# Two reorderings in one kernel: pair sums taken on VectorE before the sums with ones, and rope and root pieces taken before the next softmax step

## Chip, cores and metric

The kernel runs on one core of a Trainium2 chip. The metric is the time of one execution on the device, in microseconds (us). The engines are called by their short names: PE (TensorE, matrix products), ACT (ScalarE, activations), DVE (VectorE, elementwise), POOL (GpSimd), SP (SyncE, here only the queue that brings weights).

## What is computed

Two blocks of two layers each run on one 1024 x 1024 float32 matrix x (1024 tokens). A layer of the first block normalizes, projects, and joins three branches; a layer of the second block joins a convolution branch, a latent attention branch and a gated unit. Cut to what matters here:

```python
def hybrid_layer(x, ...):                       # first block, 2 layers
    h = rms_norm(x, norm_g); proj = h @ w_in
    # 4 heads, two score maps each, rope on part of q and k
    sc = einsum('bhcqd,bhckd->bhcqk', rotate(q), rotate(k))
    p = softmax(where(mask, sc, NEG_INF)); w = p[:, :, 0] - lam * p[:, :, 1]
    a = rms_norm(w @ v, subln_g) * (1 - lam_init) * silu(az)
    ...
def _layer(x, ...):                             # second block, 2 layers
    y = causal_conv31(a * sigmoid(a_glu)) + conv_b           # 256 channels
    y_conv = (silu(layer_norm(y)) @ pw_w + pw_b) * silu(z_conv)
    v = layer_norm(gelu(v)); y_sg = gelu(u) * mix(v) * silu(z_sg)   # 256 channels
    y = concat([rms_norm(y_conv), rms_norm(y_mla), rms_norm(y_sg)])
    return x + y @ w_out
```

## The kernel before

**Layout.** Activations lie channels first: 128 channels on the partitions, 1024 tokens along the row. A branch of 256 channels is thus two tiles of 128x1024. A sum over channels, which every norm needs, is a matmul with a matrix of ones, which adds over the 128 partitions and leaves the sum on all of them.

**Projections.** Each weight matrix is cut into panels of 1024x128. SP brings a panel, POOL splits it into a high and a low float32r part (lines 443 and 446), and PE multiplies in three passes (lines 477 for half the tokens, 496 for all of them). A panel for all tokens is 48 matmuls, one for half of them 24. Two panels are held at a time; PE's first matmul of a panel tells POOL that the other buffer may be overwritten.

**Order.** All orders are written out by hand: each engine runs its own program, and semaphores join them. In the first block's attention the loop runs over 4 heads h and 8 query tiles q. In step (h, q) PE computes the scores of the next step (lines 717, 722), then "pieces" of other work listed in B1_SLOTS, then the value products at q = 4 (line 765), then waits for `mixed` and transposes the mixed probabilities (line 701), then more pieces. Pieces are half projections of the next head's q, k and v, the gate z, and "ss", the sum of squares of a finished head's half (line 754). Pieces and transposes go in turn through a ring F of three PSUM banks. PE can fill a bank only after its last reader has freed it.

The readers are these. For q and k, DVE's `piece`: shuffle from PSUM (line 1274), product with the cosines from PSUM (line 1276, this frees the bank), product of the shuffled copy with the sines (line 1278), and their sum (line 1281). For "ss", ACT's `piece`: logarithm from PSUM (line 996, frees the bank) and exponential (line 998); DVE's part is lines 1289 and 1293. For the softmax: DVE's `maxima` (line 1253) from PSUM, ACT's `exps` (line 974), DVE's `mix` (lines 1261 to 1265), which signals `mixed`. The pieces q, k and ss that stand behind the transposes of a step are kept in a list `late` and are taken by DVE and ACT in the next step, behind `maxima` and behind `exps`.

**Second block.** After the conv panels PE runs six pair sums per layer among the panels: "cmean" and "smean" over the two tiles of conv output YC and gated input VG, "cvar" and "svar" over their squares, "cbn" and "sbn" over the squares of the two branches' outputs. Each is `pair_sum`: the two tiles one after the other into the same PSUM buffer of a ring T with two buffers. ACT writes the squares (line 2040 and 2041, semaphore sq2) and takes the roots (lines 2030 and 2033). DVE centres (lines 2303, 2305), scales (line 2293), and adds latent squares (line 2335). `total` is the same sum for one tile.

Of the kernel before, what the change touches and what calls it, by code (L numbers as in the profile page):

```python
# [33 lines left out]
HALF = SEQ // 2  # L34
# [491 lines left out]
def first_block(env):  # L526
# [3 lines left out]
    with ExitStack() as ctx:  # L530
# [424 lines left out]
        def scalar(act):  # L955
# [55 lines left out]
            def attention(L):  # L1011
# [220 lines left out]
        def vector(dve):  # L1232
# [34 lines left out]

            def piece(L, use):
                kind, h, half = use
                c, psF = slice(half * HALF, (half + 1) * HALF), bank(use)  # L1270
                if kind in ("q", "k"):
                    dst = (AQ if kind == "q" else AK)[h % 2][:, c]
                    dve.wait_ge(*F.filled(L, use))
                    step(dve.stream_shuffle(ROT, psF, exchange(8)))
                    scale = SCALE if kind == "q" else 1.0
                    dve.scalar_tensor_tensor(out=dst, in0=psF, scalar=scale, in1=rope[:, 0, c], op0=ALU.mult,  # L1276
                                             op1=ALU.mult).then_inc(F.freed(use), 1)
                    step(dve.scalar_tensor_tensor(out=ROT, in0=ROT, scalar=scale, in1=rope[:, 1, c], op0=ALU.mult,
                                                  op1=ALU.mult))
                    dve.wait_ge(*F.drained(L, use))  # L1280
                    dve.tensor_tensor(dst, dst, ROT, ALU.add).then_inc(rotated.sem, 1)
                    dve.wait_ge(*rotated.upto(L, rotations(h, kind, half)))
# [18 lines left out]
            def attention(L):  # L1301
# [11 lines left out]
                for h in range(HEADS):  # L1313
                    for q in range(NT):
                        mix(L, h, q)
                        if q + 1 < NT:
# [291 lines left out]
def second_block(env):  # L1608
# [3 lines left out]
    with ExitStack() as ctx:  # L1612
# [56 lines left out]
        kr_sq = Tally(sem("kr_sq"), 1)  # L1669
# [13 lines left out]
        SQ_C, SQ_S = [X[:, 4], X[:, 5]], [X[:, 6], X[:, 7]]  # L1683
        ROOT, ROOT_C, ROOT_S = ypad[:, 0, PAD:], wk[:, 8], wk[:, 10]
# [71 lines left out]
        def tensor(pe):  # L1756
# [25 lines left out]

            def pair_sum(L, use, tiles):

                pe.wait_ge(*T.room(L, use))
                full(psT[:, T.buf(use)], ones[:], tiles[0], True, False)
                full(psT[:, T.buf(use)], ones[:], tiles[1], False, True).then_inc(T.filled_sem, 1)
# [145 lines left out]
            for L in range(DEPTH):  # L1933
# [4 lines left out]

                pe.wait_ge(*conv_done.upto(L, 2))
                pair_sum(L, "cmean", [YC[:, 0], YC[:, 1]])  # L1940
                pe.wait_ge(*A.drained(L, ("v", 1)))
                pair_sum(L, "smean", [VG[:, 0], VG[:, 1]])
# [4 lines left out]
                pe.wait_ge(*sq2.upto(L, 2))  # L1947
                pair_sum(L, "svar", SQ_S)
# [12 lines left out]
                pe.wait_ge(*sq2.upto(L, 3))  # L1961
                pair_sum(L, "cbn", SQ_C)
# [21 lines left out]
                pe.wait_ge(*sq2.upto(L, 4))  # L1984
                pair_sum(L, "sbn", SQ_S)
# [301 lines left out]
        def vector(dve):  # L2287
# [199 lines left out]
            for L in range(DEPTH):  # L2487
# [23 lines left out]
                for m in (0, 1):  # L2511
                    dve.wait_ge(*A.filled(L, ("pw", m)))
                    dve.scalar_tensor_tensor(out=ZC[:, m], in0=psA[:, A.buf(("pw", m))], scalar=col(C2.pwb + m),
                                             in1=ZC[:, m], op0=ALU.add, op1=ALU.mult).then_inc(A.freed(("pw", m)), 1)
                dve.wait_ge(*T.filled(L, "wgt"))
# [3 lines left out]
                    .then_inc(T.freed("wgt"), 1)  # L2519
                for t in (0, 1):  # L2520
# [212 lines left out]
```

## Time and profile before

| | before |
|---|---|
| median of 3 runs | 3786.62 us (3783.96 to 3786.62) |
| profiled execution | 3790.16 us |
| its span, first to last instruction | 3788.3 us |
| PE matmul busy | 3653.4 us, 96% |
| DVE busy | 1789.2 us, 47% |
| ACT busy | 1081.0 us, 29% |
| POOL busy | 1389.4 us, 37% |
| mean granted TensorE clock | 0.989 |

Busy times are those of the profiled execution. "Granted clock" is the share of TensorE's full clock (2.4 GHz) that the chip let through. Matmuls overlap one another in the trace, so a time per matmul is better read from the distance of starts than from the duration of one. Where an engine idles, the trace names what released it.

### The profile page before, as it was taken

What the parts mean: (1) busy time and instruction counts of PE and PEld (TensorE: products, weight loads), DVE (VectorE), ACT (ScalarE), POOL (GpSimd) and SP (SyncE); (2) the same over time, 40 slices, a digit from 0 to 9 for tenths busy, and PEclk for the clock granted to TensorE, in tenths of its full rate; (3) what the DMA queues carried; (4) which work ended last, traced back from release to release, by engine and by line L of the source; (5) the groups of instructions that cost most, each with busy time, mean ns of one, the idle gap of its engine ahead of it and who ended that gap; (6) DMA issues with size and microseconds to landing.
All of it is one profiled execution on the core that took longest, in us unless ns stands there. A gap on an engine that the chain in (4) does not pass through costs nothing.

```text
span 3788.3 us, 42491 instructions
## 1 busy us (share of the span) xinstructions
PE 3653.4 (96%) x16560; PEld 2814.1 (74%) x16560; DVE 1789.2 (47%) x2208; ACT 1081.0 (29%) x1779; POOL 1389.4 (37%) x670
## 2 busy tenths in 40 slices
PE   6999999999999999999999999999999999999999
PEld 5667788887778666788887887777666678776667
DVE  4665123233145666203233235883566579446653
ACT  3334100101212334200101213123465331435542
POOL 2212344342356222344442247343422255342224
PEclk9999999999999999999999999999999999999999
DMA  4101111111124100111111114311110231111112
GB/s 152 33 23 31 53 50 48 44 49 38 35 92 141 34 28 28 46 54 50 44 50 34 39 46 139 102 40 34 45 34 23 78 124 51 29 47 32 33 65 92
DMA packets 69643, 209.22 MB, mean 55 GB/s; under 512 B 7536, under 2 KB 8560, under 8 KB 68976
## 3 DMA queue, kind: packets, MB, share of 16 engines
q1 hardware_dynamic: 48960, 159.08, 14.1%
q10 hardware_dynamic: 20528, 47.91, 3.6%
q8 instruction: 117, 1.92, 0.2%
q14 instruction: 38, 0.31, 0.0%
HBM read 185.99 MB, written 20.97 MB: 55 GB/s over the span
## 4 chain that ended last, share of the span: by engine, by line
PE 88%; DVE 8%; ACT 3%; issue 1%; DMA 0%; POOL 0%; SPq 0%; ACTq 0%; DVEq 0%; POOLq 0%
PE psA L496 45%; PE psT L477 18%; PE psA L477 7%; PE psA L1804 3%; PE psA L717 2%; PE psT L1872 2%; PE psT L1780 1%; PE psT L765 1%; PE psT L1775 1%; PE psT L701 1%; PE psT L1849 1%; DVE b_negmax L1253 1%; DVE Hlo L2298 1%; DVE b_wk L2321 1%; PE psT L1846 1%
## 5 line engine op out<-in xcount | busy, mean ns | idle before, releaser
L443 POOL TENSOR_TENSOR Whi<-stage,credit 128x1024 fp32r<-128x1024 f32 (+1 forms) x332 | 598.1, 1802 | 2353.6 <-PE psA L496 1192.7
L446 POOL TENSOR_TENSOR Wlo<-stage,Whi 128x1024 fp32r<-128x1024 f32 (+1 forms) x332 | 790.9, 2382 | 26.1
L496 PE MATMUL psA<-Hhi,Whi 128*128 128x512 f32 x2240 | 700.8, 394 | 0.4 <-DVE b_ypad L2311 0.4
L496 PE MATMUL psA<-Hlo,Whi 128*128 128x512 f32 x2240 | 690.0, 389 | 0.0
L496 PE MATMUL psA<-Hhi,Wlo 128*128 128x512 f32 x2240 | 689.8, 389 | 0.0
L496 PEld LDWEIGHTS psA<-Hhi,Whi 128*128 128x128 f32 x2240 | 419.4, 188 | 98.2 <-issue 13.0
L496 PEld LDWEIGHTS psA<-Hlo,Whi 128*128 128x128 f32 x2240 | 420.5, 188 | 88.1
L496 PEld LDWEIGHTS psA<-Hhi,Wlo 128*128 128x128 f32 x2240 | 420.5, 188 | 87.8
L477 PE MATMUL psT<-Hhi,Whi 128*128 128x512 f32 x1024 | 425.3, 415 | 46.2 <-DVE b_wk L1276 25.9
L477 PE MATMUL psT<-Hhi,Wlo 128*128 128x512 f32 x1024 | 409.3, 400 | 0.0
L477 PE MATMUL psT<-Hlo,Whi 128*128 128x512 f32 x1024 | 408.9, 399 | 0.0
L477 PEld LDWEIGHTS psT<-Hhi,Whi 128*128 128x128 f32 x1024 | 198.6, 194 | 99.2 <-issue 59.6
L2321 DVE SCALAR_TENSOR_TENSOR b_wk<-b_ypad,b_cur,b_wk 128x1024 f32<-128x1024 f32 x120 | 230.5, 1921 | 4.1
L477 PEld LDWEIGHTS psT<-Hhi,Wlo 128*128 128x128 f32 x1024 | 198.1, 193 | 44.5
L477 PEld LDWEIGHTS psT<-Hlo,Whi 128*128 128x128 f32 x1024 | 198.9, 194 | 37.9 <-issue 0.7
L477 PE MATMUL psA<-Hhi,Whi 128*128 128x512 f32 x448 | 181.3, 405 | 7.2 <-DVE Hlo L1364 6.3
L1253 DVE TENSOR_REDUCE b_negmax<-psA 128x1 f32<-128x256 f32 (+7 forms) x128 | 91.0, 753 | 182.5 <-PE psA L722 182.5
L477 PE MATMUL psA<-Hhi,Wlo 128*128 128x512 f32 x448 | 176.9, 395 | 0.0
L477 PE MATMUL psA<-Hlo,Whi 128*128 128x512 f32 x448 | 176.6, 394 | 0.0
L1082 ACT ACTIVATE b_wk<-psA 128x1024 f32<-128x1024 f32 x32 | 32.9, 1027 | 440.8 <-PE psA L496 440.8
L974 ACT ACTIVATE X<-psA,b_negmax 128x256 f32<-128x256 f32 (+7 forms) x128 | 93.9, 738 | 224.8 <-DVE b_negmax L1253 224.8
L967 ACT ACTIVATE b_wk<-psA 128x1024 f32<-128x1024 f32 x40 | 41.0, 1025 | 405.6 <-PE psA L496 405.6
(319 smaller groups left out, 4881.7 us busy)
## 6 DMA issues: line engine op xcount, KB each, us to landing
stage<-in_w SPq DMA_DIRECT2D x264, 512.0 KB, 3.5
stage<-in_w SPq DMA_DIRECT2D x68, 256.0 KB, 2.6
xs<-X ACTq DMA_DIRECT2D x8, 2048.0 KB, 8.4
b_wk<-xs ACTq DMA_DIRECT2D x32, 256.0 KB, 4.1
b_wk<-xs ACTq DMA_DIRECT2D x14, 512.0 KB, 6.2
rope<-in_ropes ACTq DMA_DIRECT2D x4, 1024.0 KB, 5.0
out<-b_wk ACTq DMA_DIRECT2D x8, 512.0 KB, 2.6
b_wk<-in_x ACTq DMA_DIRECT2D x4, 512.0 KB, 10.6
```

Of the source, the lines that this page charges most:

```text
L443: pool.tensor_tensor(Whi[:, b, 0:n], stage[:, b, 0:n], credit[:, 0:1].broadcast_to([P, n]), ALU.add).then_inc(s.w_hi, 1)
L446: pool.tensor_tensor(Wlo[:, b, 0:n], stage[:, b, 0:n], Whi[:, b, 0:n].bitcast(F32), ALU.subtract).then_inc(s.w_split, 1)
L477: mm = pe.matmul(dst[0:M], w[:, cols], r[k][:, c], start=k == 0 and w is whi and r is rhi, stop=k == nk - 1 and end)
L496: mm = pe.matmul(dst[h], w[:, cols], r[k][:, h * HALF:(h + 1) * HALF], start=first and k == order[0] and r is rhi and w is whi, stop=last ...
L701: mm = pe.transpose(dst[:, i * P:(i + 1) * P], src[:, i * P:(i + 1) * P], ident[:])
L717: pe.matmul(dst[:, k0:k1], AQ[h % 2][rows, q * P:n], AK[h % 2][rows, k0:k1], start=True, stop=k1 < n)
L967: act.activation(dst, psA[:, A.buf(use)], func).then_inc(A.freed(use), 1)
L974: act.activation(PR[q % 2][c][:, 0:n], psA[:, A.buf(use), 0:n], ACT.Exp, bias=negmax[:, q % 2, c:c + 1], accum_out=rowsum[:, q % 2, c:c + ...
L1253: dve.reduce_max(negmax[:, q % 2, c:c + 1], psA[:, A.buf(use), 0:n], AX_X, negate=True)\
L1804: pe.matmul(dst[:, k0:k1], Q[sd][:, q * P:n], keys[g][:, 0:k1 - k0], start=True, stop=k1 < n)
L1872: mm = pe.matmul(psAV[side_rows(sd), c0:], v[:, b * M_V:(b + 1) * M_V], WT[sd][:, k, c0:], start=k == 0, stop=k == 4 * g + 3)
L2321: ins = dve.scalar_tensor_tensor(out=YC[:, t], in0=ypad[:, t, k:k + SEQ], scalar=col(C2.conv_w + 2 * k + t), in1=YC[:, t], op0=ALU.mult, o ...
```

## The change

On DVE, in the first block's attention, `piece` for q and k is cut in two: `swapped` (shuffle and first product, frees the bank) and `turned` (second product and sum). For late pieces `swapped` now stands between `mix` and `maxima`, `turned` stays behind `maxima`. On ACT all late pieces (only "ss" does anything there) now stand ahead of `exps`.

In the second block each pair sum becomes one `total` of a tile that DVE has added before: PAIR_C and PAIR_S for the means (new use of wk 14 and 15), and the squares in place. A semaphore `paired` (six per layer) tells PE. The function `pair_sum` goes. The final scaling of the conv branch on DVE moves from behind the sg tiles to ahead of them.

```diff
 # ACT, first block
                 for h in range(HEADS):
                     for q in range(NT):
+                        for use in late:
+                            piece(L, use)
                         if q + 1 < NT:
                             exps(L, h, q + 1)
                         elif h + 1 < HEADS:
                             exps(L, h + 1, 0)
-                        for use in late:
-                            piece(L, use)
 # DVE, first block
+            def swapped(L, use):
+                kind, h, half = use
+                c, psF = slice(half * HALF, (half + 1) * HALF), bank(use)
+                dve.wait_ge(*F.filled(L, use))
+                step(dve.stream_shuffle(ROT, psF, exchange(8)))
+                dve.scalar_tensor_tensor(out=(AQ if kind == "q" else AK)[h % 2][:, c], in0=psF,
+                                         scalar=SCALE if kind == "q" else 1.0, in1=rope[:, 0, c], op0=ALU.mult,
+                                         op1=ALU.mult).then_inc(F.freed(use), 1)
+            def turned(L, use):
+                ...
+                step(dve.scalar_tensor_tensor(out=ROT, in0=ROT, scalar=SCALE if kind == "q" else 1.0,
+                                              in1=rope[:, 1, c], op0=ALU.mult, op1=ALU.mult))
+                dve.wait_ge(*F.drained(L, use))
+                dve.tensor_tensor(dst, dst, ROT, ALU.add).then_inc(rotated.sem, 1)
+                dve.wait_ge(*rotated.upto(L, rotations(h, kind, half)))
 ...
                         mix(L, h, q)
+                        for use in late:
+                            if use[0] != "ss":
+                                swapped(L, use)
                         if q + 1 < NT:
                             maxima(L, h, q + 1)
                         elif h + 1 < HEADS:
                             maxima(L, h + 1, 0)
                         for use in late:
-                            piece(L, use)
+                            if use[0] == "ss":
+                                piece(L, use)
+                            else:
+                                turned(L, use)
 # PE, second block (likewise for smean, svar, sbn)
-                pe.wait_ge(*conv_done.upto(L, 2))
-                pair_sum(L, "cmean", [YC[:, 0], YC[:, 1]])
+                pe.wait_ge(*paired.upto(L, 1))
+                total(L, "cmean", PAIR_C)
-                pe.wait_ge(*sq2.upto(L, 1))
-                pair_sum(L, "cvar", SQ_C)
+                pe.wait_ge(*paired.upto(L, 3))
+                total(L, "cvar", SQ_C[0])
-                pe.wait_ge(*sq2.upto(L, 3))
-                pair_sum(L, "cbn", SQ_C)
+                pe.wait_ge(*paired.upto(L, 5))
+                total(L, "cbn", SQ_C[0])
 # DVE, second block
                 taps(L, 1, 12, CONV_K)
+                dve.wait_ge(*conv_done.upto(L, 2))
+                dve.tensor_tensor(PAIR_C, YC[:, 0], YC[:, 1], ALU.add).then_inc(paired.sem, 1)
+                dve.wait_ge(*A.drained(L, ("v", 1)))
+                dve.tensor_tensor(PAIR_S, VG[:, 0], VG[:, 1], ALU.add).then_inc(paired.sem, 1)
                 centre(L, "cmean", YC)
                 centre(L, "smean", VG)
                 add_latent(L, 1)
+                for n, pair in ((1, SQ_C), (2, SQ_S)):
+                    dve.wait_ge(*sq2.upto(L, n))
+                    dve.tensor_tensor(pair[0], pair[0], pair[1], ALU.add).then_inc(paired.sem, 1)
 ...
+                dve.wait_ge(*sq2.upto(L, 3))
+                dve.tensor_tensor(SQ_C[0], SQ_C[0], SQ_C[1], ALU.add).then_inc(paired.sem, 1)
                 dve.wait_ge(*T.filled(L, "wgt"))
 ...
+                dve.wait_ge(*roots.upto(L, 3))
+                for m in (0, 1):
+                    scale_by(ZC[:, m], C2.bn + m, ROOT_C).then_inc(c_fin.sem, 1)
                 for t in (0, 1):
                     dve.wait_ge(*A.filled(L, ("sg", t)))
 ...
-                dve.wait_ge(*roots.upto(L, 3))
-                for m in (0, 1):
-                    scale_by(ZC[:, m], C2.bn + m, ROOT_C).then_inc(c_fin.sem, 1)
+                dve.wait_ge(*sq2.upto(L, 4))
+                dve.tensor_tensor(SQ_S[0], SQ_S[0], SQ_S[1], ALU.add).then_inc(paired.sem, 1)
```

## Rows read from the trace of the kernel before

**Rows 1.** Windows: us, busy by engine (x instructions), PEclk, DMA share, GB/s.
```profile
80.00:400.00 320.00, 301.60 (x1375) 214.69 (x1373) 185.08 (x283) 118.99 (x244) 75.13 (x34) 0.98 0.11 31
2520.00:2690.00 170.00, 168.73 (x736) 127.78 (x735) 77.31 (x51) 71.53 (x67) 59.61 (x27) 1.00 0.12 38
```

**Rows 2.** PE's waits, 80 to 400 us: us in total, times, longest.
```profile
PE psT L477 <- DVE b_wk L1276: 12.7, 8, 2.5
PE psT L477 <- ACT b_upad L996: 3.0, 3, 1.0
...
PE psT L701 <- DVE X L1265: 0.8, 1, 0.8
```

**Rows 3.** Timeline (start, us, engine, line, operation, [idle before]), around one wait.
```profile
249.78 1.02 DVE L1253 TENSOR_REDUCE b_negmax<-psA 128x1 f32<-128x384 f32 x2 [10.10 <-PE psA L722]
...
250.73 0.72 DVE L1274 STREAM_SHUFFLE b_upad<-psT 128x512 f32<-128x512 f32 x1
...
251.49 0.69 DVE L1276 SCALAR_TENSOR_TENSOR b_wk<-psT,rope 128x512 f32<-128x512 f32 x1
...
252.33 0.47 PE L477 MATMUL psT<-Hhi,Whi 128*128 128x512 f32 x1 [1.92 <-DVE b_wk L1276]
```

**Rows 4.** Timeline, first head, from the z projection to the transposes of step 5.
```profile
124.72 0.47 PE L477 MATMUL psT<-Hhi,Whi 128*128 128x512 f32 x1 [0.64 <-DVE b_wk L1276]
...
128.30 2.83 DVE L1265 SCALAR_TENSOR_TENSOR X<-X,b_inv 128x768 f32<-128x768 f32 x1
...
132.20 0.82 PE L701 MATMUL psT<-ident,X 128*128 128x128 f32 x6
```

**Rows 5.** Timeline, second head, step 3 and the second half of k.
```profile
183.60 2.39 POOL L446 TENSOR_TENSOR Wlo<-stage,Whi 128x1024 fp32r<-128x1024 f32 x1
...
183.62 2.92 DVE L1278 SCALAR_TENSOR_TENSOR b_upad<-b_upad,rope 128x512 f32<-128x512 f32 x1
...
188.27 0.75 DVE L1265 SCALAR_TENSOR_TENSOR X<-X,b_inv 128x512 f32<-128x512 f32 x1
...
192.26 0.47 PE L477 MATMUL psT<-Hhi,Whi 128*128 128x512 f32 x1 [2.52 <-DVE b_wk L1276]
```

**Rows 6.** Single lines over the span: duration min/median/max ns, first and last start.
```profile
L1278 DVE SCALAR_TENSOR_TENSOR b_upad<-b_upad,rope x32: 682/683/2919, 55.9 to 1440.1; 128x512 f32<-128x512 f32 x32
...
L1276 DVE SCALAR_TENSOR_TENSOR b_wk<-psT,rope x32: 691/692/692, 55.3 to 1439.5; 128x512 f32<-128x512 f32 x32
...
L2335 DVE TENSOR_TENSOR b_ypad<-b_ypad,b_wk x10: 1224/1227/3462, 2538.3 to 3334.8; 128x1024 f32<-128x1024 f32 x10
```

**Rows 7.** Timeline, the root of a head sum and the projection behind it.
```profile
149.70 0.69 ACT L996 ACTIVATE b_upad<-psT,epsc 128x512 f32<-128x512 f32 x1
...
150.53 0.47 PE L477 MATMUL psT<-Hhi,Whi 128*128 128x512 f32 x1 [1.01 <-ACT b_upad L996]
```

**Rows 8.** Windows: two half projections, and two slices of 20 us.
```profile
98.40:104.10 5.70, 5.67 (x26) 4.48 (x26) 3.20 (x7) 0.00 (x0) 0.00 (x0) 1.00 0.01 3
172.30:179.70 7.40, 7.33 (x26) 5.64 (x26) 3.24 (x7) 0.00 (x0) 0.00 (x0) 0.77 0.00 1
...
160.00:180.00 20.00, 18.08 (x74) 13.02 (x74) 5.67 (x12) 2.27 (x7) 4.28 (x2) 0.91 0.09 27
...
1420.00:1440.00 20.00, 17.21 (x74) 11.56 (x73) 15.55 (x25) 5.99 (x13) 1.67 (x1) 0.91 0.08 27
```

**Rows 9.** Timeline of PE, second block: the sums cmean and smean, and the next panel.
```profile
2529.01 7.03 PE L1775 MATMUL psT<-b_wk,ones 128*128 128x512 f32 x16
2535.47 0.79 PE L496 MATMUL psA<-Hhi,Whi 128*128 128x512 f32 x1
```

**Rows 10.** Timeline: ACT's root behind the sum cbn, and the transposes that wait for it.
```profile
2585.96 1.11 ACT L2030 ACTIVATE b_wk<-psT,epsc 128x1024 f32<-128x1024 f32 x1 [1.11 <-PE psT L1775]
...
2587.22 1.06 PE L1780 MATMUL psT<-ident,b_wk 128*128 128x128 f32 x8 [0.42 <-ACT b_wk L2030]
```

**Rows 11.** Timeline of DVE: the last two operations of the convolution, layer 0.
```profile
2525.22 2.60 DVE L2321 SCALAR_TENSOR_TENSOR b_wk<-b_ypad,b_cur,b_wk 128x1024 f32<-128x1024 f32 x2
```

More of the change, by code:

```diff
@@ L1266, in mix @@
                     .then_inc(mixed.sem, 1)
+            def swapped(L, use):
[7 more added lines that the diff above has]
+            def turned(L, use):
+                kind, h, half = use
+                c = slice(half * HALF, (half + 1) * HALF)
+                dst = (AQ if kind == "q" else AK)[h % 2][:, c]
+                step(dve.scalar_tensor_tensor(out=ROT, in0=ROT, scalar=SCALE if kind == "q" else 1.0,
[3 more added lines that the diff above has]
+                dve.wait_ge(*rotated.upto(L, rotations(h, kind, half)))
             def piece(L, use):
@@ L1271, in piece @@
                 if kind in ("q", "k"):
[L1272 to L1282, printed above, removed]
+                    swapped(L, use)
+                    turned(L, use)
                 elif kind == "vt":
@@ L1315, in attention @@
                         mix(L, h, q)
+                        for use in late:
+                            if use[0] != "ss":
+                                swapped(L, use)
                         if q + 1 < NT:
@@ L1320, in attention @@
                         for use in late:
-                            piece(L, use)
+                            if use[0] == "ss":
+                                piece(L, use)
+                            else:
+                                turned(L, use)
                         done, late = late, []
@@ L1668, in second_block @@
         c_fin, s_fin = Tally(sem("c_fin"), 2), Tally(sem("s_fin"), 2)
-        kr_sq = Tally(sem("kr_sq"), 1)
+        kr_sq, paired = Tally(sem("kr_sq"), 1), Tally(sem("paired"), 6)
         q_rs, k_rs = Tally(sem("q_rs"), 2 * M_HEADS), Tally(sem("k_rs"), 2 * M_HEADS)
@@ L1683, in second_block @@
         SQ_C, SQ_S = [X[:, 4], X[:, 5]], [X[:, 6], X[:, 7]]
+        PAIR_C, PAIR_S = wk[:, 14], wk[:, 15]
         ROOT, ROOT_C, ROOT_S = ypad[:, 0, PAD:], wk[:, 8], wk[:, 10]
@@ L1781, in turn @@
                 return mm
[L1783 to L1787, printed above, removed]
             def total(L, use, sums):
@@ L1936, in tensor @@
                     panel(L, name)
-                pe.wait_ge(*conv_done.upto(L, 2))
-                pair_sum(L, "cmean", [YC[:, 0], YC[:, 1]])
-                pe.wait_ge(*A.drained(L, ("v", 1)))
-                pair_sum(L, "smean", [VG[:, 0], VG[:, 1]])
+                pe.wait_ge(*paired.upto(L, 1))
+                total(L, "cmean", PAIR_C)
+                pe.wait_ge(*paired.upto(L, 2))
+                total(L, "smean", PAIR_S)
                 panel(L, ("cq", 2))
-                pe.wait_ge(*sq2.upto(L, 1))
-                pair_sum(L, "cvar", SQ_C)
-                pe.wait_ge(*sq2.upto(L, 2))
-                pair_sum(L, "svar", SQ_S)
+                pe.wait_ge(*paired.upto(L, 3))
+                total(L, "cvar", SQ_C[0])
+                pe.wait_ge(*paired.upto(L, 4))
+                total(L, "svar", SQ_S[0])
                 panel(L, ("cq", 3))
@@ L1983, in tensor @@
                 panel(L, ("cq", 4))
-                pe.wait_ge(*sq2.upto(L, 4))
-                pair_sum(L, "sbn", SQ_S)
+                pe.wait_ge(*paired.upto(L, 6))
+                total(L, "sbn", SQ_S[0])
                 panel(L, ("cq", 5))
```

## The prediction

> **What bounds the kernel now.** I read the page first, then the granted clock and the busy time by stage, then who PE (TensorE) waits for, then the timeline around each kind of wait. PE is busy for 96% of the span. In the stretch of the second block that the change touches it is busy for 168.73 of 170 us, in the attention stage of the first block only for 301.60 of 320 us [rows 1]. So there are two ways to save time: less PE work where PE never rests, and fewer PE waits in the first block's attention. In the latter the reader is to see two names in the list of waits: 12.7 us in 8 waits for line 1276, the DVE (VectorE) operation that frees the PSUM bank of a q or k projection, and 3.0 us in 3 waits for line 996, the ACT (ScalarE) operation that frees the bank of a head sum [rows 2]. The same list for the second layer (1240 to 1560 us) has the same two totals. Together 2 x 15.7 = 31.4 us. DVE is busy for 185 of the 320 us there, so it is no bound on the average, but it may be one for a step.
>
> **Change, part 1: half of the rope goes ahead of the row maxima.** Nothing is added; the order on DVE changes. Now DVE does mix, maxima, then the shuffle and the first product (lines 1274, 1276), and PE, which wants the bank, stands still until the product ends [rows 3]. There maxima begin at 249.78 because the scores end then, DVE having idled 10.1 us. The projection was complete before those scores (PE's program has it ahead of them, some 1.2 us of scores later). In the new order the shuffle and product, 1.45 us, run during the scores, so the bank is free at about 250.2, and PE wanted it at 252.33 - 1.92 = 250.41. The wait goes whole; maxima start some 0.4 us later, ahead of a 5.7 us projection that hides this. The in-loop waits are three kinds, each counted over both layers: six of 1.92 us as here, six of 0.64 us (the one at 124.72 in [rows 4]), four of 2.52 us [rows 5], in all 11.5 + 3.8 + 10.1 = 25.4 us. In the 0.64 kind of the first head DVE idles before its maxima, so that wait goes too.
>
> The 2.52 kind is tighter. DVE's mix ends at 188.27 + 0.75 = 189.02, the product would then end at 190.47, and PE is ready at 192.26 - 2.52 = 189.74 [rows 5]: by these rows 0.9 us would stay. But mix is itself late, since line 1278 took 2.92 us beside POOL's weight split where its median is 0.68 us [rows 5, 6]. With the product early, line 1278 starts about 1 us sooner relative to the projection, inside POOL's first operation instead of its second; its partner 1281 is then held by the second one. I put mix 0.65 us earlier and the remaining wait at 0.25 us (bounds 0 and 0.9), four times: 1.0 us lost. The same shift shortens PE's two waits of 0.8 us for mix (line 1265) [rows 2] to about 0.3 us: 1.0 us gained.
>
> What is late next: the two SBUF-only operations that stay behind the maxima (1278, 1281). In heads 1 and 2 PE will reach step 4 some 4 us sooner (no 2.52 us wait, no slow clock), DVE will not. Those two operations then begin after POOL's split has begun, which starts soon after the z projection. In the first head the last mix operation of step 5 ends at 128.30 + 2.83 = 131.13, which is 6.4 us after the projection's start, and PE wants it at 132.20, 7.5 us after it [rows 4]. With two more operations held I get 8.0 us: a new wait of 0.5 us, in two heads and two layers, 2.0 us (bounds 0 and 2.2 us each, one held operation: 2.92 - 0.68).
>
> The Trainium skill (SBUF — State Buffer, section "Who interferes with whom") says that a DVE instruction with two SBUF inputs and a GpSimd instruction that reads SBUF exclude each other for a whole instruction, and that one with a single SBUF input does not contend. The trace agrees: 2.92 against 0.68 us for line 1278, while line 1276, which reads PSUM, has 691 to 692 ns in all its 32 cases [rows 6]. The rule speaks against a part of this change, since exactly the operations that can be held are left behind the maxima; it is the ground of a rival below.
>
> **Part 2: root of a head sum ahead of the next exponentials.** ACT now takes the exponentials first and then line 996, 0.69 us, and PE waits 1.01 us [rows 7]; six times over both layers, 6.0 us. PE computes the sum ahead of the scores, and ACT has nothing to do until the maxima of these scores are there, so the bank is free before PE asks at 149.52. The exponentials start some 0.5 us later. The wait goes whole. What ACT has queued behind the wait for the sum is the exponentials alone, and PE's program has the sum ahead of their scores, so no new stall.
>
> Waits of part 1 and 2: 31.4 - 1.0 - 2.0 + 1.0 = **29.4 us**.
>
> **Clock.** After six of the ten waits of 1.92 or 2.52 us the granted clock fell. The projection at 172.30 took 7.40 us for 26 matmuls at 0.77, the one at 98.40 took 5.70 us for 26 at 1.00 [rows 8]: 1.7 us. The six are in the 20 us slices of 160, 180, 260, 1320, 1340 and 1420 us, all at 0.91 with no other wait of size in them (the first and the last of them in [rows 8]). Where the waits go I let these go: 6 x 1.7 = **10.2 us** (bounds 0 and 10.8, by 0.09 x 20 us each).
>
> The Trainium skill (TensorE: Matmul & The Clock Gate, section "What's actually happening") has it that the engine is slow by default and activity releases it, at points that do not follow the program. The trace agrees, equal waits of 1.92 us being followed by the lower level (1.2 GHz) at one place and not at another. By that rule dips at waits that remain may come or go as well.
>
> **Part 3: pair sums.** Six sums per layer in the second block went over two tiles, four matmuls each, and each float32 matmul stands in the trace as two records. Two pair sums, 16 records, take from 2529.01 to 2535.47, 0.43 us from one to the next [rows 9]. One tile instead of two drops 4 records per sum, 24 per layer, 10.3 us, and PE is full there, so it all counts: 20.6 us. Of this, back: the sum "cbn" is followed by ACT's root, which has its table loaded at 2585.96 - 1.11 = 2584.85 [rows 10]. With the sum 1.7 us earlier the root begins there, only 1.1 us earlier, and the transposes that wait for it follow: 0.6 us a layer, 1.2 in all.
>
> The added DVE work is six 128x1024 additions per layer, 1.22 us each alone and up to 3.46 us beside POOL [rows 6]. Covers: the first stands right behind the convolution, which ends at 2525.22 + 2.60 = 2527.82 [rows 11]. POOL idles there, so it ends at about 2529.1, PE being ready at 2529.0: 0.25 us lost with the semaphore, in layer 0 (in layer 1 DVE is further ahead). The second runs beside the first sum. The additions of squares have an 11 us projection panel ahead of their sums; even at 3.46 us each they end 2 us before PE asks. Losing that cover would cost up to 3 us each. Moving the conv branch's final scaling ahead of the sg tiles fills time in which DVE idles and frees the place behind them. The new waits on DVE hold only work that itself needed the same squares or PE's later output.
> Part 3: 20.6 - 1.2 - 0.25 = **19.2 us** (bounds 14 and 20.6).
>
> **Sum.** 29.4 + 10.2 + 19.2 = 58.8 us. The profiled execution took 3790.16 us (span 3788.3): 3731.4. The median of the runs is 3786.62, 3.5 us below it: **3727.8 us**.
>
> **Rivals.**
> A. The clock gives nothing back: dips appear at other waits in the place of those six. For: they did not follow every equal wait. Against: the new waits are below 1 us. 3727.8 + 10.2 = 3738 us.
> B. The softmax chain becomes the bound in the heavy steps (2 to 4 of heads 1 and 2, both layers, 12 steps): one held operation each, 2.24 us less some 0.4 of slack, 1.8 x 12 = 22 us: 3750 us. For: PE already waits 0.8 us for mix once a layer. Against: the order within a step only permutes the same DVE work.
> C. Part 1 frees a bank that was not what PE lacked: the next release (weights, or scores) is as late, and of the 39.6 us of waits and clock little comes. Only part 3 stays: 3786.6 - 19.2 = 3767 us. Against: POOL's split ends at 183.60 + 2.39 = 185.99, and PE comes for the bank only at 189.74 [rows 5].
> D. Slower. In all 24 in-loop steps with a rope piece both lines 1278 and 1281 are pushed into POOL's split and held, 2 x 2.24 = 4.5 us, with the mix and PE's transposes behind them: 108 us back, 3728 + 108 = 3836 us. It decides the sign from 58.8 / 24 = 2.45 us per step that reach PE. For: the 2.92 us row. Against: POOL splits a panel in only about half of these steps, and DVE idles ahead of most maxima, 10.1 us at 249.78 [rows 3].
>
> **How the numbers follow.** Forecast 0.70, A 0.12, B 0.08, C 0.05, D 0.05. The range reaches to A and most of the way to B: up 10.2 us (clock) and 8 us (mix waits at their upper bound), 3746; down about 12 us, if dips at other waits go as well, each worth 1.7 us or more, 3716. A measurement of this kernel can tell 0.2% (7.6 us) from no change. Faster 0.95, same 0.01, slower 0.04: all cases but D are faster by over 0.2%; a D reduced to near its deciding point gives the 0.01.
>
> **What would show it.** Right: line 1276 and line 996 gone from PE's waits in the loop (two short prelude waits may stay), line 1265 small and perhaps at new places; slices of 20 us at 0.91 gone in the stage 80 to 400; records of the sums 48 fewer; a wait under 0.5 us for the first addition; about 1.1 and 1 us waits at the transposes behind cbn. Wrong: PE waits of 1 us and more for mix in heads 1 and 2, waits for an addition of squares, or the same number of clock dips elsewhere.

## The result, and the profile after

The changed kernel takes **3730.62 us** (median; runs 3725.36 to 3733.77), the kernel before took 3786.62. Ratio 0.9852, 95% interval 0.9840 to 0.9863: 56 us less. The prediction was 3727.8 us (3716 to 3746), faster. The profiled execution of the changed kernel took 3733.77 us, with a span of 3731.9; the one before had 3788.3, so the two traces differ by 56.4 us.

The line numbers moved: the first product is line 1274 (was 1276), the second 1283 (was 1278), the sums with ones are at 1794 (was 1775), the transposes of block 2 at 1799 (was 1780), the root's logarithm at 2043 (was 2030).

Windows of the changed kernel, first attention stage and a stretch of block 2 with the sums (columns as in [rows 1]):

```profile
80.00:400.00 320.00, 315.81 (x1464) 227.88 (x1463) 189.34 (x287) 123.98 (x250) 85.19 (x40) 0.99 0.12 37
2470.00:2640.00 170.00, 168.11 (x747) 130.88 (x746) 95.77 (x60) 69.17 (x64) 63.34 (x28) 0.99 0.13 41
```

In [rows 1] PE was busy for 301.60 of the first 320 us; now it is 315.81. In block 2 it was full before and is full now: there the gain is in work that is gone, not in waits. The page's first part says the same, with 48 matmul records fewer than the 16560 of before:

```profile
PE 3623.8 (97%) x16512; PEld 2798.9 (75%) x16512; DVE 1812.8 (49%) x2220; ACT 1081.7 (29%) x1779; POOL 1392.4 (37%) x670
```

What PE waits for between 80 and 400 us, the list that answers to [rows 2]:

```profile
PE psA L717 <- ACT X L974: 1.8, 1, 1.8
PE psT L477 <- DVE b_wk L1274: 1.2, 2, 0.6
PE psT L754 <- ACT b_upad L1009: 0.8, 1, 0.8
PE psT L701 <- DVE X L1265: 0.4, 1, 0.4
```

Twelve waits with 16.5 us (12.7, 3.0 and 0.8) have become three with 1.6 us. The first and third line are a prelude and an end that the change doesn't touch. The waits that are left, in the timeline:

```profile
110.94 0.66 PE L701 MATMUL psT<-ident,X 128*128 128x128 f32 x4 [0.41 <-DVE X L1265]
181.88 0.47 PE L477 MATMUL psT<-Hhi,Whi 128*128 128x512 f32 x1 [0.58 <-DVE b_wk L1274]
252.40 0.47 PE L477 MATMUL psT<-Hhi,Whi 128*128 128x512 f32 x1 [0.58 <-DVE b_wk L1274]
```

The two of 0.58 us are the successors of the 2.52 us kind of [rows 5]. No row shows the wait for mix in step 5 of the second and third head that I had foreseen.

**Where the time went, by stage.** The trace can be cut at waits that every version has (the 1.85 us wait of line 717 opens an attention stage, the 0.78 us wait of line 754 closes it; the stretches of block 2 with the convolution and the sums begin at the wait for the convolution's input in layer 0 and at the 2.66 us wait of the layer's norm in layer 1, and end at the 0.88 us wait for the latent vectors). For each stretch I add up (1 - granted clock) x length over slices of 5 us: the time that the lower clock level cost, in brackets. A dip, one spell at the lower level (1.2 GHz), shows as 1.7 us in this count. The count takes every dip as paid in full, which is not always so (last section).

| kernel | attention, layer 0 | attention, layer 1 | conv and sums, layer 0 | conv and sums, layer 1 | all the rest |
|---|---|---|---|---|---|
| before | 314.63 (6.80) | 314.63 (6.80) | 260.97 (0) | 315.17 (1.70) | 2582.9 (26.0) |
| after | 292.92 (1.70) | 292.90 (1.70) | 253.16 (1.70) | 305.54 (1.70) | 2587.4 (30.2) |
| after, clock taken out | 291.2 | 291.2 | 251.5 | 303.8 | 2557.2 |
| gain, clock taken out | 16.6 | 16.6 | 9.5 | 9.6 | -0.3 |

The gains add up to 52.0 us. Clock losses fell from 41.3 to 37.0 us in all, 4.3 us more: 56.3 of the 56.4 us. The traces are one execution each, so the split of the clock between stages is that of two draws; the lengths with the clock taken out repeat from version to version.

### The profile page after: what moved, and what is told of

It reads as the page before. It is cut to its first block, busy times and chain, and to the rows that moved or that the text cites. A ratio compares the mean times of both kernels' runs of the same rounds, so it can differ in the third digit from the quotient of the medians.

```text
span 3731.9 us, 42407 instructions
## 1 busy us (share of the span) xinstructions
PE 3623.8 (97%) x16512; PEld 2798.9 (75%) x16512; DVE 1812.8 (49%) x2220; ACT 1081.7 (29%) x1779; POOL 1392.4 (37%) x670
## 3 DMA queue, kind: packets, MB, share of 16 engines
q1 hardware_dynamic: 48960, 159.08, 14.4%
q8 instruction: 117, 1.92, 0.2%
HBM read 185.99 MB, written 20.97 MB: 55 GB/s over the span
## 4 chain that ended last, share of the span: by engine, by line
PE 88%; DVE 7%; ACT 3%; issue 1%; DMA 0%; POOL 0%; SPq 0%; ACTq 0%; DVEq 0%; POOLq 0%
PE psA L496 46%; PE psT L477 17%; PE psA L477 7%; PE psA L1817 3%; PE psT L1885 2%; PE psT L765 2%; PE psA L717 2%; PE psT L1799 1%; PE psT L701 1%; PE psT L1862 1%; DVE Hlo L2311 1%; DVE b_wk L2334 1%; PE psT L1859 1%; PE psT L496 1%; PE psT L1794 1%
## 5 line engine op out<-in xcount | busy, mean ns | idle before, releaser
L443 POOL TENSOR_TENSOR Whi<-stage,credit 128x1024 fp32r<-128x1024 f32 (+1 forms) x332 | 595.6, 1794 | 2294.4 <-PE psA L496 1179.2
```

Source lines behind the costliest of these rows:

```text
L443: pool.tensor_tensor(Whi[:, b, 0:n], stage[:, b, 0:n], credit[:, 0:1].broadcast_to([P, n]), ALU.add).then_inc(s.w_hi, 1)
```

## Experiments

**Part 1 alone (rope ahead of the maxima).** The kernel before with DVE's new order only:

```
                         mix(L, h, q)
+                        for use in late:
+                            if use[0] != "ss":
+                                swapped(L, use)
                         (maxima of the next step)
                         for use in late:
-                            piece(L, use)
+                            (ss: piece, else: turned)
```

> The kernel before with part 1 alone (shuffle and first product of late q and k pieces ahead of the maxima). Theory 1, the parts add and each wait costs more than its idle time: in the changed kernel the attention stages shrank by 21.7 us each, of which six waits for the root (1.01 us each, about 0.2 us more for the restart of the matmul pipeline) are not in this kernel: 2 x 21.7 - 7.3 = 36 us less, 3750.5 us. PE waits for line 996 six times 1.01 us in the loop, for line 1276 four times about 0.6 us. Rival A, the clock dips only move: the same waits go, but dips appear elsewhere, 25 to 30 us less, 3757 to 3761 us. Rival B, the softmax chain takes over: waits for line 1265 of 1 us and more, 3765 us or more.

Measured: 3754.46 us, ratio 0.9913 (0.9897 to 0.9930). Of PE's waits between 80 and 400 us the two that are new or changed (line 996 still has its 3.0 us in 3), and three rows of the timeline:

```profile
PE psT L701 <- DVE X L1265: 1.2, 3, 0.4
PE psT L477 <- DVE b_wk L1274: 1.2, 2, 0.6
...
187.97 0.69 DVE L1310 TENSOR_TENSOR b_Blo<-b_upad,b_Bhi 128x512 fp32r<-128x512 f32 x1 [0.70 <-ACT b_Bhi L1003]
...
199.01 1.02 DVE L1265 SCALAR_TENSOR_TENSOR X<-X,b_inv 128x768 f32<-128x768 f32 x1
...
200.09 0.88 PE L701 MATMUL psT<-ident,X 128*128 128x128 f32 x6 [0.39 <-DVE X L1265]
```

The attention stages take 297.80 (1.70) and 297.79 (1.70) us: clock taken out, 11.7 us less each, and 5.1 us less clock loss each. Outside the stretches of the table the loss grew, 31.4 us against 26.0, so the clock cost 36.5 us in the whole trace instead of the 31.1 that were left if only the six dips had gone. The median is 4 us above the theory's 3750.5; the profiled execution is itself 3.7 us above that median, so its clock doesn't show why. And here the wait that I had foreseen exists: PE waits 0.39 us for mix at 200.09 and again at 272.46, in the second and the third head, for which I had put 0.5.

**Part 2 alone (root ahead of the exponentials).** The kernel before with ACT's new order only:

```
+                        for use in late:
+                            piece(L, use)
                         (exponentials of the next step)
-                        for use in late:
-                            piece(L, use)
```

> The kernel before with part 2 alone (late pieces ahead of the exponentials on ACT). Theory 1: six waits of 1.01 us for line 996 go, with 0.2 us of restart each: 7.3 us less, 3779.3 us; the waits for line 1276 stay at 25.4 us and the dips behind them too. Rival: the exponentials begin later and PE's wait for mix takes the place: no change, 3786.6 us, with waits for line 1265.

Measured: 3774.72 us, ratio 0.9976 (0.9967 to 0.9986), 4.6 us below the theory. The three waits for line 996 are gone from the list, and the others stand as they were, the largest among them:

```profile
PE psT L477 <- DVE b_wk L1274: 12.7, 8, 2.5
```

The attention stages take 307.60 (3.40) and 307.66 (3.40) us. Clock taken out that is 3.6 us a stage for three waits of 1.01 us. Besides, 3.4 us of clock loss went in each stage, though every one of the 1.92 and 2.52 us waits is still there. That is 6.8 us of clock that the theory didn't have. So a dip doesn't belong to one wait: with the same waits there are two fewer in each stage. The 6.8 us needn't be the edit's: the ten runs lie between 3770.93 and 3784.62 us, at granted clocks from 0.992 to 0.988.

Together, parts 1 and 2 alone give 15.3 us a stage (11.7 + 3.6), and both at once 16.6. The 1.3 us are, to 0.1 us, the two 0.39 us waits for mix of part 1 alone, with the 0.2 us that each wait costs beyond its idle (below).

**Part 3 alone (pair additions).** The kernel before with the second block of the changed one:

```
+ dve.tensor_tensor(pair[0], pair[0], pair[1], ALU.add)    (six per layer)
- full(psT, ones, tiles[0], True, False); full(psT, ones, tiles[1], False, True)
+ full(psT, ones, sums)
```

> The kernel before with part 3 alone (pair sums added on DVE, and the scaling moved). Theory 1: 24 records of 0.43 us less per layer, 0.6 us a layer back behind cbn: 19.4 us less, 3767 us; between milestones of PE in layer 1 without a dip 9.6 us less. Rival, clock dips eat it: 15 us or less, 3771 us or more, with the sum of (1 - granted clock) over the span higher than before's by 4 us. Rival, DVE late: waits of PE for the additions of over 1 us each.

Measured: 3770.96 us, ratio 0.9958 (0.9941 to 0.9975). The stretches with the sums take 251.58 (0) and 305.56 (1.70) us: 9.4 and 9.6 us less, as in the changed kernel. The median is only 14.4 us below that of before on the same chip (3785.36), and here the clock rival holds in part. The sums gave their 19.0 us, as the two stretches show, but the four runs have a granted clock of 0.989 each where the 13 runs of before on that chip average 0.9904, which over 3769 us is some 5 us more loss. The two traces hide it (42.1 us of loss against 41.3), because the profiled execution of before, at 0.989, was itself among the slower in clock. Whether the edit brings such executions or four runs happened to fall so isn't shown.

**The whole rope piece ahead of the maxima.** The changed kernel, with the second product and the sum moved as well. This puts to the test whether DVE's operations are in the way of the softmax chain (rival B):

```
                         for use in late:
                             if use[0] != "ss":
-                                swapped(L, use)
+                                piece(L, use)
                         (maxima of the next step)
                         for use in late:
                             if use[0] == "ss":
                                 piece(L, use)
-                            else:
-                                turned(L, use)
```

> The changed kernel with the whole rope piece (all four DVE operations) ahead of the maxima instead of half of it. Theory of held operations (a DVE operation with two SBUF inputs waits for POOL's split): the two SBUF-only products now run before POOL's split begins, so line 1278 never takes 2.9 us and mix of step 3 is earlier; the 0.58 us waits in heads 1 and 2 and the 0.4 us waits for mix shrink or go: 3727 to 3731 us, 0 to 3 us less than the changed kernel. Rival B, the order on DVE is what counts: maxima 1.4 us later in all 24 steps put exponentials and mix late, PE waits for line 1265 in heavy steps: 5 to 15 us more, 3736 to 3746 us.

Measured: 3721.46 us, ratio 0.9830 (0.9813 to 0.9846), 9 us below the changed kernel. PE's waits between 80 and 400 us:

```profile
PE psA L717 <- ACT X L974: 1.8, 1, 1.8
PE psT L754 <- ACT b_upad L1009: 0.8, 1, 0.8
```

The attention stages take 290.59 (1.70) and 289.00 (0) us, 2.3 and 2.2 us less than in the changed kernel with the clock taken out. More DVE work ahead of the maxima made no new wait and removed the last three. Rival B is out: the softmax chain has slack for all four operations (0.74, 0.69, 0.68 and 0.69 us, 2.8 together). Splitting the piece, as the change does, is worse than moving all of it. Of the 14.0 us between the two traces 8.6 are clock, 28.4 us of loss in the whole trace against 37.0.

**GpSimd's subtraction made short.** The kernel before; is it the held products (2.92 us in [rows 5]) that make PE wait?

```
-  pool.tensor_tensor(Wlo[:, b, 0:n], stage[:, b, 0:n], Whi[:, b, 0:n], ALU.subtract)
+  pool.tensor_tensor(Wlo[:, b, 0:P], stage[:, b, 0:P], Whi[:, b, 0:P], ALU.subtract)
```

> The kernel before, with GpSimd's subtraction that makes the low part of the weights done for the first 128 of a panel's columns only (the rest of the low part stays zero, so the part of the product that low weights bring is left out for the other columns): GpSimd's 2.4 to 3.5 us operation becomes about 0.3 to 0.5 us. Theory (VectorE's 0.68 us products of the rope piece are held to 2.92 us while GpSimd's low subtraction runs): the products at L1278 and L1281 stay at 0.7 to 1.2 us in all calls, the 1.92 and 2.52 us waits of TensorE at L1276 in heads 1 to 3 vanish or fall below 0.6, waits at L1276 between 80 and 400 us fall from 12.7 us to under 4, and the time falls by 20 to 60 us to 3725 to 3767 (GpSimd frees VectorE in other stages too). Rival (the products are long for another reason: the PSUM read beside ScalarE's, or GpSimd's high copy): some products at L1278 still take 2.5 us or more, waits at L1276 stay above 8 us.

Measured: 3761.35 us, ratio 0.9934 (0.9914 to 0.9954). The low part of the other columns stays at zero (it is cleared once at the start, not shown), so this kernel leaves out their share of the product. The lines are one further down here. First the two operations over the span (minimum, median, maximum in ns), then PE's wait list of the attention stage, then the timeline at the place of [rows 5]:

```profile
L447 POOL TENSOR_TENSOR Wlo<-stage,Whi x332: 454/465/1530, 19.5 to 3738.4; 128x128 fp32r<-128x128 f32 x166
...
L1279 DVE SCALAR_TENSOR_TENSOR b_upad<-b_upad,rope x32: 682/683/1228, 54.4 to 1429.2; 128x512 f32<-128x512 f32 x32
...
PE psT L478 <- DVE b_wk L1277: 13.0, 8, 2.7
...
181.20 0.46 POOL L447 TENSOR_TENSOR Wlo<-stage,Whi 128x128 fp32r<-128x128 f32 x1
181.22 0.99 DVE L1279 SCALAR_TENSOR_TENSOR b_upad<-b_upad,rope 128x512 f32<-128x512 f32 x1
...
189.86 0.47 PE L478 MATMUL psT<-Hhi,Whi 128*128 128x512 f32 x1 [2.67 <-DVE b_wk L1277]
```

Half of my expectation fell. The hold is what I took it for: the product that took 2.92 us beside a 2.39 us subtraction takes 0.99 beside one of 0.46. The Trainium skill (SBUF — State Buffer, section "Who interferes with whom") has the two exclude each other for a whole instruction, and the trace agrees: in both rows the product ends 0.55 us after the subtraction does (186.54 against 185.99 in [rows 5], 182.21 against 181.66 here), so it ran behind it. But the waits for the first product stay, 13.0 us in 8 and the longest 2.67 us. They come from the order on DVE alone. What went is the 0.8 us wait for mix (line 1265), as it is the held product that made mix late; the attention stages are 0.9 and 0.7 us shorter with the clock taken out. The rest of the 25 us is gained outside the attention stages. In the wait list of the whole span the waits for the split state of line 1364 fell from 6.3 to 1.9 us, and two of 3.5 us without a releaser are gone, each with a 0.9 us wait and 3.4 us of clock loss beside it. The two stretches around these, from the 0.85 us wait behind cbn to the 0.45 us wait of the latent projections, went from 120.7 to 113.3 and from 120.8 to 113.3 us, which is 15 of the 25. What makes up the last few stays open.

**TensorE shifted by a few matmuls.** Are the clock's dips tied to certain waits? The changed kernel, with the last token tile's transposes near 65 us repeated:

```
+                    if t == NT - 1:
+                        turn(psA[:, t % 2], XT[t], KT)
+                        turn(psA[:, t % 2], XT[t], KT)
                     turn(psA[:, t % 2], XT[t], KT).then_inc(x_turned, 1)
```

> The changed kernel, with the eight transposes pairs of the last token tile made three times instead of once near 65 us (16 matmul records, 1.77 us, each time): 3.54 us more work for TensorE, nothing else changed, so every later instruction comes 3.54 us later against the clock gate's own beat. Theory (the stretches of about 20 us at granted clock 0.91 fall where a wait of about 1 us meets the gate at the wrong moment, so a shift re-deals them): waits at the same lines with the same sizes as in the changed kernel, but other 20 us slices at 0.91; the time is 3730.6 + 3.5 plus or minus 1.7 for each dip dealt anew, so anywhere in 3727 to 3741, and the stages that gain or lose a dip change by 1.7 us each. Rival (dips belong to particular waits of this kernel): the same slices at 0.91, shifted by 3.5 us, and 3734.1 within 0.7.

And with four extra copies:

> As e7_shift, with four extra copies of the last token tile's transposes: 7.08 us more work near 65 us. Theory (dips dealt by phase): 3737.7 plus or minus 1.7 for each dip, so 3731 to 3745, and a pattern of 0.91 slices that is neither that of the changed kernel nor that of e7_shift. Rival (dips belong to particular waits): 3737.7 within 0.7 and the same slices shifted by 7 us.

Measured: 3728.86 us, ratio 0.9849 (0.9833 to 0.9865), with two copies and 3733.35 us, 0.9858 (0.9841 to 0.9874), with four. My count of the added work was twice too high: 8 records make one copy, and the row of line 701 grows from 2.01 us (16 records) to 3.75 and 5.50 us, so the shifts are 1.75 and 3.5 us. PE's waits in the first attention stage are those of the changed kernel to 0.1 us. The dips are not:

| kernel | attention 0 | attention 1 | conv and sums 0 | conv and sums 1 | clock loss in all |
|---|---|---|---|---|---|
| after | 292.92 (1.70) | 292.90 (1.70) | 253.16 (1.70) | 305.54 (1.70) | 37.0 |
| two copies | 291.29 (0) | 292.87 (1.70) | 251.57 (0) | 305.54 (1.70) | 33.1 |
| four copies | 292.99 (1.70) | 291.33 (0) | 251.63 (0) | 307.15 (3.35) | 36.5 |

With the clock taken out each stage agrees within 0.2 us over the three kernels. The rival (dips belong to particular waits) put 3.5 and 7 us for the added work; corrected to 1.75 and 3.5 us it would give 3732.4 and 3734.1, and the first is missed by 3.5 us, which is about what the clock gave back (33.1 against 37.0). The table doesn't show that the shift moved them: it compares one execution of each kernel, and executions of unshifted code differ as much (below). Windows 80 to 100 us, changed kernel and two copies; both have the 1.85 us wait of line 717 in it, at 86.06 and 87.47:

```profile
80.00:100.00 20.00, 18.16 (x86) 13.66 (x85) 12.41 (x27) 4.20 (x16) 4.27 (x2) 0.91 0.27 78
...
80.00:100.00 20.00, 18.15 (x93) 13.81 (x92) 13.08 (x30) 4.37 (x17) 4.27 (x2) 1.00 0.31 88
```

The same is seen without any added work. The 1.11 us wait of line 695 is followed by a dip in the changed kernel and by none in the version with the whole rope piece ahead; here their windows 860 to 880 us and PE's rows behind that wait, in this order:

```profile
860.00:880.00 20.00, 18.89 (x77) 13.55 (x76) 5.55 (x7) 1.26 (x2) 2.81 (x2) 0.91 0.09 27
876.10 3.63 PE L695 MATMUL psT<-b_upad,ones 128*128 128x512 f32 x4 [1.11 <-ACT b_upad L1096]
...
860.00:880.00 20.00, 18.89 (x84) 14.24 (x84) 7.05 (x7) 3.21 (x3) 4.41 (x3) 1.00 0.08 27
873.55 1.99 PE L695 MATMUL psT<-b_upad,ones 128*128 128x512 f32 x4 [1.11 <-ACT b_upad L1096]
```

The plainest case needs no edit in the stage at all. The kernel with part 3 alone has the first block of the kernel before, and its twelve waits of attention 0 are those of before to 0.01 us. Yet the clock cost 3.4 us there and 6.8 in before. Its row of a 2.52 us wait, the window around it, and the window around the same wait in before (192.26 in [rows 5]):

```profile
189.61 0.47 PE L477 MATMUL psT<-Hhi,Whi 128*128 128x512 f32 x1 [2.52 <-DVE b_wk L1276]
180.00:200.00 20.00, 17.28 (x82) 11.81 (x80) 17.11 (x27) 6.83 (x16) 3.26 (x2) 1.00 0.08 27
...
180.00:200.00 20.00, 17.48 (x75) 12.24 (x73) 15.86 (x25) 5.81 (x13) 4.28 (x2) 0.91 0.10 27
```

In the same way attention 1 of the version with the scaling put back, whose first block is that of the changed kernel, takes 291.32 (0) us against 292.90 (1.70). So a wait of 1 to 2.5 us makes a dip possible and not certain, and the same wait in the same code is followed by one in one execution and by none in another. What decides it no run here shows. The Trainium skill (TensorE: Matmul & The Clock Gate, section "What's actually happening") says that the release comes at points that do not follow the program; the traces agree, the same code with the same waits having 6.8 us of dips in one execution and 3.4 in another.

**The scaling put back.** The changed kernel with the convolution's final scaling behind the sg tiles again:

```
-                dve.wait_ge(*roots.upto(L, 3))
-                for m in (0, 1):
-                    scale_by(ZC[:, m], C2.bn + m, ROOT_C)...
                 for t in (0, 1):
                     (sg tiles)
+                (the three lines)
```

> The changed kernel with the scaling of the convolution's output (two products with the root for cbn) put back behind the two sg tiles on VectorE, where it stood before. Theory (that move gains nothing, since nobody waits for the scaled tiles for a long time, and the gain of block 2 comes from the 48 matmul records alone): each of the two convolution stages of block 2 as long as in the changed kernel within 0.3 us once the granted clock is taken out (251.5 and 303.8 us), time 3726 to 3735. Rival (the move lets the branch's last sum of squares go earlier, and without it TensorE waits for the addition behind s_out): a new wait of 0.5 to 3 us at the sum for sbn in each layer, 3731 to 3741.

Measured: 3727.75 us, ratio 0.9847 (0.9819 to 0.9876). The stretches take 251.58 (0) and 307.18 (3.40) us, so 251.6 and 303.8 with the clock taken out, against 251.5 and 303.8. That move is worth nothing.

**A faster version.** The whole rope piece ahead of the maxima, and in block 2 ScalarE takes zm0 behind the root for cbn and the two copies:

```
+                root(L, "cbn", ROOT_C, 1.0 / 256, roots.sem)
+                (the two vst copies)
                 take(L, ("zm", 0), ZM[:, 0], ACT.Silu)
-                root(L, "cbn", ROOT_C, 1.0 / 256, roots.sem)
-                (the two vst copies)
```

> e4_whole (the whole rope piece of the half panel ahead of the next maxima) with one more order changed: in block 2 ScalarE makes the root for cbn and the two vst copies ahead of taking the zm0 panel, so that the logarithm need not stand behind the 1.02 us take and a 1.28 us table load. Theory: the 1.04 us wait at the vst transposes of the changed kernel shrinks by about 0.65 us in both layers, all else as in e4_whole: 3720.2, with dips of 1.7 us each dealt anew, so 3717 to 3725. Rival (the late take of zm0 makes the sg tile wait for its room, or moves the whole tail of block 2 later): 3723 to 3728, with a new wait before L1992 or at the panel behind it.

Measured: 3721.84 us, ratio 0.9829 (0.9813 to 0.9846). First the rows of the changed kernel behind the sum cbn, then those of this version:

```profile
2537.36 1.28 ACT L2041 ACT_TABLE_LOAD   x1
2538.65 1.11 ACT L2043 ACTIVATE b_wk<-psT,epsc 128x1024 f32<-128x1024 f32 x1
2539.91 1.06 PE L1799 MATMUL psT<-ident,b_wk 128*128 128x128 f32 x8 [1.04 <-ACT b_wk L2043]
2541.82 1.12 PE L1982 MATMUL psT<-ident,b_small 128*128 128x128 f32 x4 [0.85 <-ACT b_wk L2238]
...
2530.71 1.11 ACT L2041 ACTIVATE b_wk<-psT,epsc 128x1024 f32<-128x1024 f32 x1 [7.95 <-PE psT L1792]
2531.97 1.06 PE L1797 MATMUL psT<-ident,b_wk 128*128 128x128 f32 x8 [0.42 <-ACT b_wk L2041]
2533.88 0.66 PE L1980 MATMUL psT<-ident,b_small 128*128 128x128 f32 x4 [0.85 <-ACT b_wk L2235]
```

The table load no longer stands between the take and the logarithm, and the wait is 0.42 us again, as in [rows 10]. The stretches are 0.6 us shorter each with the clock taken out (250.97 and 303.24 against 251.55 and 303.85). The median doesn't show it: the clock cost 33.3 us in this trace and 28.4 in that of the version it is built on. The two versions can't be told apart by time, and both beat the changed kernel by some 9 us.

## Why the prediction was right, point by point

**Waits in the first block.** I had 29.4 us of removed waits. The idle removed is 15.0 us in each layer (16.56 to 1.56), 30.0 in all, and the sum was right by its parts going both ways. The remaining wait of the 2.52 us kind is 0.58 us instead of 0.25 (four times over both layers, 1.3 us too little). The remaining wait for mix is 0.41 us instead of 0.3, and in the first head. The new wait for mix, 0.5 us four times, isn't there; it is there, with 0.39 us, when part 1 stands alone. Part 2 takes it away. The same place in the changed kernel:

```profile
186.73 0.69 DVE L1310 TENSOR_TENSOR b_Blo<-b_upad,b_Bhi 128x512 fp32r<-128x512 f32 x1 [0.70 <-ACT b_Bhi L1003]
...
198.17 1.02 DVE L1265 SCALAR_TENSOR_TENSOR X<-X,b_inv 128x768 f32<-128x768 f32 x1
...
199.28 0.84 PE L701 MATMUL psT<-ident,X 128*128 128x128 f32 x6
```

The root isn't only what frees PE's bank, it also starts the head-sum piece on DVE, whose last operation (line 1310) starts earlier than with part 1 alone. Counted from PE's 0.58 us wait just before, at 181.88 here and at 182.15 there, it starts after 4.85 us instead of 5.82, and mix ends after 17.3 instead of 17.9. So mix ends at 199.19, and PE comes at 199.28. I had judged the parts one at a time: of part 2 I had counted the bank and not the work that follows the root.

**What I left out: a wait costs more than its idle.** The stages became 16.6 us shorter with the clock taken out for 15.0 us of idle. Nine waits fewer: 1.6 / 9 = 0.18 us each. Part 2 alone gives (3.6 - 3.0) / 3 = 0.2, the whole piece ahead (18.9 - 16.56) / 12 = 0.2, part 1 alone (11.71 - 11.17) / 4 = 0.14. Over 18 waits it is 3.2 us, which I didn't have. Some of it is in the rows: the first matmul behind a wait takes 0.47 us where its kind has 0.39 to 0.41. What makes up the rest no row shows.

**Clock: the term that was mis-sized.** The six dips in the attention stages are gone as I said, 5.1 us in each layer. But 10.2 us is not what the kernel got back: 4.3. Elsewhere dips came at waits that had been followed by none: 1.7 us behind line 695 in layer 0 and 3.4 in layer 1, which the change doesn't touch, and 1.7 at the transposes behind cbn; one of 1.7 us went in block 2's attention. That is rival A by its mechanism (dips appear at other waits), in about half its size. Two things say that even 4.3 is loose. The six dips were those of one trace: with part 3 alone the same twelve waits of attention 0 had one dip behind them and not three. And over all runs with a listed clock, 23 of the kernel before and four of the changed one, the mean granted clock is 0.9904 and 0.9905, where 10 us given back would have made 0.993; the listed values are rounded to 0.001, so this is rough. The step that failed is "Where the waits go I let these go", which took a dip as the property of a wait. A dip that can fall on any wait of 1 to 2.5 us is to be counted by the number of such waits that are left, and in this kernel most are left.

**Sums.** I had 19.2 us, the stretches show 19.1 (9.5 and 9.6). Its parts: the rows give 0.40 us a record (6.46 us for 16, [rows 9]), not the 0.43 that I wrote, and the version without the loss behind cbn gains 10.0 and 10.2 us for 24 records, 0.42 each. The loss behind cbn was put at 0.6 us a layer and is 0.6, with waits of 1.04 and 0.85 us as foreseen. No wait for an addition shows at all, the 0.25 us for the first one included. The row of the pair sum shows that it needn't: cmean and smean now take 3.1 us, and PE goes on without idling:

```profile
2489.55 3.70 PE L1794 MATMUL psT<-b_wk,ones 128*128 128x512 f32 x8
2492.68 1.03 PE L496 MATMUL psA<-Hhi,Whi 128*128 128x512 f32 x2
```

**The rivals.** B (the softmax chain bound in heavy steps) falls with the version that puts still more ahead of the maxima and has no wait left. C (the wrong releaser) falls with part 1 alone, which removes the waits it names. D (both operations behind the maxima held in all 24 steps): the trace after has no step where PE waits over 0.6 us in the loop. Held operations exist, and the one thing they cost PE was the 0.8 us wait for mix.

**The total.** 58.8 us forecast, 56.4 between the traces: waits 29.4 against 33.2 (3.2 of it the cost beyond the idle), clock 10.2 against 4.3, sums 19.2 against 19.1. So the total is near partly by luck: two terms were off in opposite directions.

## What to carry to other kernels

An operation that only frees another engine's buffer goes ahead of one that must wait for that engine, the whole of its piece rather than half of it if the queue has the slack, and the list of waits shows before the edit what it is worth (idle plus some 0.2 us a wait here). Count a clock dip as a chance that comes with each wait of 1 to 2.5 us, not as part of the price of the wait that it happened to follow. Judge an edit by the length of the stretch it touches with the clock taken out, since the median of the whole kernel moves by as much from dips elsewhere as from a small edit.

## What the runs showed that I had not expected

**A dip can be free.** In block 2's attention the changed kernel has one dip less (8.50 us of clock loss against 10.25), and yet that stretch is no shorter, 387.83 against 387.65 us. PE's rows before (first two) and after (last two), with the windows between them:

```profile
2950.11 0.55 PE L1780 MATMUL psT<-ident,b_wk 128*128 128x128 f32 x3 [1.35 <-DVE b_wk L2451]
2953.83 0.99 PE L1780 MATMUL psT<-ident,b_wk 128*128 128x128 f32 x4 [0.17 <-DVE b_wk L2451]
2950.00:2954.00 4.00, 3.30 (x9) 1.65 (x10) 3.93 (x8) 2.19 (x6) 0.00 (x0) 0.64 0.54 199
...
2903.30 0.55 PE L1799 MATMUL psT<-ident,b_wk 128*128 128x128 f32 x3 [1.63 <-DVE b_wk L2464]
2907.01 0.66 PE L1799 MATMUL psT<-ident,b_wk 128*128 128x128 f32 x4 [1.62 <-DVE b_wk L2464]
2903.20:2907.00 3.80, 1.95 (x8) 1.00 (x8) 3.73 (x8) 1.77 (x4) 0.00 (x0) 1.00 0.50 174
```

From one transpose group to the next it is 3.72 us at a granted clock of 0.64 and 3.71 us at 1.00. DVE is what the second group waits for, so at full clock PE only waits longer, 1.62 us instead of 0.17. That is the 1.9 us by which "all the rest", with the clock taken out, seems to lose in this stretch; small gains elsewhere hide it in the table.

**The spread of the runs.** The four runs of the changed kernel lie between 3725.36 and 3733.77 us, with granted clocks from 0.992 down to 0.989. One more dip is 1.7 us, and 8 us of spread are five of them. The version with only the scaling put back has the changed kernel's waits to within some 2 us in all, and its trace has 26.8 us of clock loss against 37.0: of two kernels that differ in nothing that matters one can look 9 us faster in a single execution (3724.68 against 3733.77).
